# Half-tile hand-offs in attention, a re-ordered last expert quad and norm, and a ring of 19 in the second expert layer

## What is computed

```
h = concat(meta, x)                                     # 272 x 1024
layer 0: h += conv_and_gated_linear_attention(rms_norm(h))
         h += moe(rms_norm(h))
layer 1: h  = h[16:] + grouped_query_attention(rms_norm(h))   # 16 heads, 4 kv heads, 272 keys
         h += moe(rms_norm(h))
out = rms_norm(h)                                       # 256 x 1024
moe: 32 experts in 4 groups; a token takes its best group and that group's two best experts
     out += gate * (silu(x @ w_gate[e]) * (x @ w_up[e])) @ w_down[e]      # 1024 -> 256 -> 1024
```

## Time and profile before

| | us |
|---|---|
| median of 3 runs (762.96, 763.95, 767.34) | 763.95 |
| the profiled execution, its own time | 761.59 |
| its span, first to last instruction | 759.7 |
| TensorE busy | 646.2 (85%) |
| VectorE busy | 250.0 (33%) |
| ScalarE busy | 172.8 (23%) |
| moved by DMA | 233.91 MB, mean 308 GB/s |
| mean granted TensorE clock | 0.937 of full |

### The profile page before, as it was taken

One profiled execution on the slowest core, in us unless ns is written; L12 is line 12 of the kernel. 1 busy time (PEld: TensorE's weight loads), 2 busy tenths in 40 slices (PEclk: granted clock), 3 DMA queues, 4 the chain that ended last, 5 costly groups with the idle time before them and its releaser, 6 DMA issues.

```text
span 759.7 us, 10990 instructions
## 1 busy us (share of the span) xinstructions
PE 646.2 (85%) x4720; PEld 398.5 (52%) x4720; DVE 250.0 (33%) x575; ACT 172.8 (23%) x354; POOL 61.4 (8%) x43
## 2 busy tenths in 40 slices
PE   3999999988899998699589988787899787686674
PEld 3896987346566373374224345466566353244231
DVE  5255434133122332033043677713213221211204
ACT  5653350031200010010005346713111000000002
POOL 4222260000000000000003420000000000000000
PEclk9999999997999999699799999999899988888888
DMA  9760345991999999999994322069999999999991
GB/s 300 272 219 1 125 125 176 374 421 62 408 422 402 423 420 421 422 420 422 417 395 156 112 75 92 1 198 424 368 424 420 420 421 421 421 420 421 421 392 63
DMA packets 45753, 233.91 MB, mean 308 GB/s; under 512 B 4432, under 2 KB 4688, under 8 KB 23168
## 3 DMA queue, kind: packets, MB, share of 16 engines
q1 hardware_dynamic: 44864, 232.34, 76.5%
q0 software_dynamic: 832, 0.76, 0.7%
HBM read 232.02 MB, written 1.05 MB: 307 GB/s over the span
## 4 chain that ended last, share of the span: by engine, by line
PE 66%; DMA 18%; DVE 6%; SPq 4%; ACT 3%; issue 2%; DVEq 0%; ACTq 0%
PE bank L1711 11%; DMA ring<-in_moe_w_up 10%; PE bank L1775 8%; DMA tail<-in_moe_w_up 7%; PE bank L1800 7%; PE bank L1748 5%; PE bank L1408 5%; PE bank L1409 4%; PE bank L1410 4%; PE bank L1762 4%; SPq L370 4%; PE bank L1617 4%; PE bank L1863 4%; ACT scratch L832 2%; PE bank L1870 1%
## 5 line engine op out<-in xcount | busy, mean ns | idle before, releaser
L1711 PE MATMUL bank<-ring,hnT 128*32 128x256 f32 (+1 forms) x1616 | 141.5, 462 | 56.5 <-DMA ring<-in_moe_w_up 24.8
L1711 PEld LDWEIGHTS bank<-ring,hnT 128*32 128x32 f32 x1616 | 70.7, 128 | 120.8 <-issue 50.9
L1800 PE MATMUL bank<-moe_scratch 128*128 128x512 f32 (+1 forms) x160 | 78.1, 611 | 1.8 <-ACT moe_scratch L739 1.6
L1192 DVE TENSOR_TENSOR moe_scratch<-moe_scratch,bank 128x256 f32<-128x256 f32 x16 | 6.7, 421 | 182.4 <-ACT moe_scratch L733 182.4
L1172 DVE TENSOR_TENSOR h<-bank,h 128x512 f32<-128x512 f32 (+1 forms) x80 | 55.1, 689 | 23.7 <-PE bank L1800 23.7
L1775 PE MATMUL bank<-sel,hn 128*128 128x256 f32 x240 | 59.1, 406 | 0.0
L1748 PE MATMUL bank<-ring,moe_scratch 128*32 128x512 f32 x496 | 58.2, 595 | 0.3 <-ACT moe_scratch L735 0.3
L1775 PEld LDWEIGHTS bank<-sel,hn 128*128 128x128 f32 x240 | 58.0, 337 | 0.0
L1800 PEld LDWEIGHTS bank<-moe_scratch 128*128 128x128 f32 (+1 forms) x160 | 22.7, 169 | 50.3 <-issue 26.3
L1408 PE MATMUL bank<-hnT_hi,mix_hi 128*128 128x272 f32 x160 | 47.1, 294 | 1.7 <-DVE scratch L1016 1.7
L733 ACT ACTIVATE moe_scratch<-bank 128x256 f32<-128x256 f32 x16 | 6.1, 384 | 186.0 <-PE bank L1711 186.0
(11 more groups left out here) (291 smaller groups left out, 852.0 us busy)
## 6 DMA issues: line engine op xcount, KB each, us to landing
ring<-in_moe_w_down SPq DMA_DIRECT2D x62, 1024.0 KB, 25.9
ring<-in_moe_w_up SPq DMA_DIRECT2D x48, 1024.0 KB, 24.2
ring<-in_moe_w_gate SPq DMA_DIRECT2D x46, 1024.0 KB, 22.1
ring<-in_sc_w_in SPq DMA_DIRECT2D x12, 1024.0 KB, 12.5
tail<-in_moe_w_gate SPq DMA_DIRECT2D x10, 1024.0 KB, 26.2
tail<-in_moe_w_up SPq DMA_DIRECT2D x8, 1024.0 KB, 25.4
ring<-in_moe_w_gate SPq DMA_DIRECT2D x14, 512.0 KB, 9.3
ring<-in_moe_w_up SPq DMA_DIRECT2D x14, 512.0 KB, 10.1
```

Of the source, the lines that this page charges most:

```text
L1711: return mm(bank[at, :], xT[:, c, mine], right, start=(c == 0), stop=(c == KC - 1))
L1800: mm(B[[7, 4][k % 2]][0:m, :], selgT[:, TILE_AT[t]:TILE_AT[t] + m], y[:, half, :], start=True, stop=True).then_inc(sem(f"sc_ps{l}"), 1)
```

## The change

1. **Ring of layer 1.** `RING` becomes [18, 19]. The token arrays `h` and `hn` are laid side by side, with the meta tokens' tile last in `h` and first in `hn` (`ROW = [2, 1, 0]`), so that these two rows' columns form one 1 MB slot, number 18, which is unit 0 of layer 1. It is loaded once `rstd_att` is known, after which layer 1 uses meta rows no more.
2. **Last quad** (both layers). `scatter(q - 1)` and its additions come between the gate and the up products of the last quad. The last scatter goes tile by tile.
3. **Attention.** Scores, maxima, exponentials and reciprocal with scalings are handed over per query tile, in two halves; the order of the three engines' lists changes, and `att_values(p-1)` comes ahead of `turn_probs(p)`.
4. **Final norm.** In halves of 512 columns, with four output transfers of 256 KB in place of two of 512 KB; the epsilon is the root's bias.

```
-    RING, HOME = 18, 16
+    RING, HOME, SIDE = [18, 19], 16, 2
...
-                  [4, 5, 3, 8, 9, 10, 11, 12, 13, 14, 15, 6, 7, 16, 17, 0, 1, 2]]
+                  [18, 4, 5, 3, 8, 9, 10, 11, 12, 13, 14, 15, 6, 7, 16, 17, 0, 1, 2]]
...
+        with ExitStack() as both:
+            rows = both.enter_context(nc.sbuf_tensor("rows", [P, 6 * D], f32))
...
+        slots.append(rows[:, 2 * D:4 * D])
...
             def first_units1():
+                sp.wait_ge(sem("rstd_att"), 1)
+                unit(1, 0)
                 wait_mix_read(sp, 1, 2)
-                for i in range(3):
+                for i in range(1, 4):
                     unit(1, i)
                 sp.wait_ge(sem("oT_ps"), 8)
-                for i in range(3, 11):
+                for i in range(4, 12):
                     unit(1, i)
                 wait_mix_read(sp, 1, NMIX[1] - 2)
-                for i in range(11, 15):
+                for i in range(12, 16):
                     unit(1, i)
                 wait_mix_read(sp, 1, NMIX[1] - 1)
-                for i in range(15, 18):
+                for i in range(16, 19):
                     unit(1, i)
...
+                first = RING[l]
+                for i in range(first, NU):
+                    if i == first or stage_of(i - first) != stage_of(i - first - 1):
+                        sp.wait_ge(sem(f"stage_done{l}"), stage_of(i - first) + 1)
                     unit(l, i)
...
             for i in range(2):
-                sp.wait_ge(sem("hn_ready"), HN_BEFORE[4] + i + 1)
-                sp.dma_start(out[0, i * P:(i + 1) * P, :], hn[:, 1 + i, :]).then_inc(sem("out_done"), 16)
-            sp.wait_ge(sem("out_done"), 32)
+                for half in range(2):
+                    cols = slice(half * W, half * W + W)
+                    sp.wait_ge(sem("hn_ready"), HN_BEFORE[4] + 2 * i + half + 1)
+                    sp.dma_start(out[0, i * P:(i + 1) * P, cols], hn[:, 1 + i, cols]).then_inc(sem("out_done"), 16)
+            sp.wait_ge(sem("out_done"), 64)
...
+        def scattered(q, tiles):
+            if q < NQ - 1:
+                return [(half, t) for half in range(2) for t in tiles]
+            return [(half, t) for t in tiles for half in range(2)]
...
+                if n == 4:
+                    done = steps * NQ * 4 + (NQ - 1) * 4
+                    for i, t in enumerate(tiles):
+                        for half in range(2):
+                            act.wait_ge(sem("h_added1"), done + 2 * i + half + 1)
+                            cols = slice(half * W, half * W + W)
+                            nc.scalar.activation(hn[:, t, cols], h[:, ROW[t], cols], ACT.Square,
+                                                 accum_out=(stats[:, 4, 0, t:t + 1], half_ss[:, t:t + 1])[half]).then_inc(sem("norm_ss"), 1)
+                            if i == 1:
+                                act.wait_ge(sem("norm_var"), upto(4) + half + 1)
+                                of = slice(tiles[half], tiles[half] + 1)
+                                nc.scalar.activation(stats[:, 4, 2, of], stats[:, 4, 1, of], ACT.Sqrt,
+                                                     bias=eps_bias[:, 0:1], scale=1.0 / D).then_inc(sem("norm_std"), 1)
+                    return
...
-            exps(0)
+            exps(0, 0)
+            exps(0, 1)
             qT_out(1)
             for p in range(8):
-                if p < 7:
-                    exps(p + 1)
-                pT_out(p)
                 if p:
                     oT_out(p - 1)
+                if p < 7:
+                    exps(p + 1, 0)
+                pT_out(p)
+                if p < 7:
+                    exps(p + 1, 1)
...
+            def last_norm():
...
+                total(0)
+                invert_root(4, 0)
+                dve.wait_ge(sem("gain_in"), 32)
+                scaled(0, 0)
+                total(1)
+                scaled(0, 1)
+                invert_root(4, 1)
+                scaled(1, 0)
+                scaled(1, 1)
...
                     for q in range(NQ):
+                        if q == NQ - 1:
+                            add_tokens(base, q - 1)
                         dve.wait_ge(sem(f"silu{l}"), base + q + 1)
                         nc.vector.tensor_tensor(he, act_g, B[2][:, F:2 * F], ALU.mult).then_inc(sem(f"he{l}"), 1)
-                        if q:
+                        if 0 < q < NQ - 1:
                             add_tokens(base, q - 1)
...
-            invert(0)
-            qT_out(1)
             for p in range(8):
+                normalize(p, 0)
+                if p:
+                    meta_out(p - 1)
                 if p < 7:
-                    maxima(p + 1)
-                if p >= 2:
-                    oT_low(p - 2)
+                    maxima(p + 1, 0)
+                normalize(p, 1)
+                if p == 0:
+                    qT_out(1)
+                if p:
+                    oT_low(p - 1)
                 if p < 7:
-                    invert(p + 1)
-                meta_out(p)
-            oT_low(6)
+                    maxima(p + 1, 1)
+            meta_out(7)
             oT_low(7)
...
                     q = NQ - 1
-                    gate_up(r, q)
+                    gate_up(r, q, (0,))
+                    scatter(r, q - 1)
+                    gate_up(r, q, (1,))
                     he_transposes(r, q)
-                    scatter(r, q - 1)
                     transpose_weights(r, q)
                     down(r, q)
                     scatter(r, q)
...
             for p in range(8):
                 if p < 7:
-                    att_scores(p + 1)
-                turn_probs(p)
+                    att_scores(p + 1, 0)
                 if p:
                     att_values(p - 1)
+                if p < 7:
+                    att_scores(p + 1, 1)
+                turn_probs(p)
             att_values(7)
```

More of the change, by code:

```diff
@@ L83, in last_user @@
     def last_user(l, slot):
-        return max(i for i in range(NU) if RING_ORDER[l][i % RING] == slot)
+        return max(i for i in range(NU) if RING_ORDER[l][i % RING[l]] == slot)
     def landed(stage):
@@ L916, in _ @@
             link(nc.vector.memset(hn[:, 0, :], 0.0))
+            nc.vector.memset(eps_bias[:, :], EPS)
             nc.vector.memset(stats[:, :, :, :].rearrange("p a b c -> p (a b c)"), 1.0).then_inc(sem("clear"), 1)
             nc.vector.memset(z[:, :, :].rearrange("p a b -> p (a b)"), 0.0).then_inc(sem("clear"), 1)
-            norm(0)
+            first_norm()
             transposes_out(0)
@@ L1165, in add_tokens @@
                 def add_tokens(base, q):
[L1167 to L1168 removed]
+                    for k, (half, t) in enumerate(scattered(q, tiles)):
                         n = TILE_N[t]
                         dve.wait_ge(sem(f"sc_ps{l}"), (base + q) * nadd + k + 1)
[L1171 removed]
+                        hh = h[0:n, ROW[t], half * W:(half + 1) * W]
                         nc.vector.tensor_tensor(hh, B[[7, 4][k % 2]][0:n, :], hh, ALU.add).then_inc(sem(f"h_added{l}"), 1)
@@ L1368, in _ @@
                     dve.wait_ge(sem("proj_ps"), PROJ["out1"] + k + 1)
-                    hh = h[:, 1 + i, half * W:(half + 1) * W]
+                    hh = h[:, ROW[1 + i], half * W:(half + 1) * W]
                     nc.vector.tensor_tensor(hh, B[k][:, :], hh, ALU.add).then_inc(sem("h_mixed1"), 1)
             moe(1)
-            norm(4)
+            last_norm()
         @block.tensor
@@ L1653, in turn @@
                         for c in range(4):
-                            last = nc.tensor.transpose(turn_place(n, i, half)[:, c, :], h[0:m, t, 4 * half + c:D:KC], ident[0:m, 0:m])
+                            last = nc.tensor.transpose(turn_place(n, i, half)[:, c, :], h[0:m, ROW[t], 4 * half + c:D:KC], ident[0:m, 0:m])
                         last.then_inc(sem("hnT_ps"), 1)
@@ L1699, in arrived @@
                     pe.wait_ge(sem(f"weights{l}_{stage % NSEM}"), r * per + count)
-                    return [RING_ORDER[l][i % RING] for i in range(NU) if stage_of(i) == stage]
+                    return [RING_ORDER[l][i % RING[l]] for i in range(NU) if stage_of(i) == stage]
                 def wait_x(r, n):
@@ L1720, in first_gate_up, with gate_up @@
                     last.then_inc(sem(f"stage_done{l}"), 1)
-                def gate_up(r, q):
-                    for u in range(2):
+                def gate_up(r, q, parts=(0, 1)):
+                    for u in parts:
                         if q == 1 or q % 2 == 0:
@@ L1790, in scatter @@
                     pe.wait_ge(sem(f"selgT{l}"), r * NQ + q + 1)
-                    for k in range(nadd):
-                        half, t = k // NT, tiles[k % NT]
+                    for k, (half, t) in enumerate(scattered(q, tiles)):
                         m = TILE_N[t]
-                        if k == 0:
+                        if half == 0:
                             pe.wait_ge(sem(f"y_act{l}"), r * NQ + q + 1)
```

(15 more changed lines are left out.)

140 lines of the change are left out of this document (71 added, 69 removed).

## The result

| kernel | median, us | executions |
|---|---|---|
| before | 763.69 | 8, 759.52 to 767.34 |
| changed | 757.58 | 8, 754.66 to 761.90 |

The account below looks back on a forecast made before the run. Experts were taken as bound by the weight stream, attention by VectorE and ScalarE alternating, the end by norm and output transfer. Gains 3.7 + 6.1 + 2.5 + 0 + 1.3 = 13.6 us off 763.95 gave 750.3 us, range 746 to 757.

Parts of the forecast that it names:

- Layer 0's last quad: Scatter fills TensorE's wait before the up products; down products then wait for their last matrix until 387.1; gain 3.7 us.
- rival (e): Little is left: attention period near 5 us, down products at the lower clock in both layers; about 761 us; chance 0.03.
- Layer 1's last quad: Down products start at most 1.9 us earlier, but idling some 4 us lowers the clock and costs 1.9; gain 0.
- Rival (b): The clock holds in layer 1's last down product, or falls only briefly; 748.4 us; chance 0.15.
- Attention: Working in halves shortens the period and the end, less a loss at the first pair; gain 6.1 us.
- The steady period: Attention's time per pair falls from 5.02 to 4.3 us; over 7 periods this gains 5.0 us.
- the end: Attention from the start of the last turn_probs to the last values: 3.2 us instead of 5.6, gaining 2.4.
- rival (a): Attention finds a new wait: 4.7 us a pair, saving 3.3 us; kernel takes 753.1 us; chance 0.20.
- The start term: Attention's first pair gives back 1.3 us: its first turn_probs stands behind a maxima half, a second reciprocal and hops.
- The ring: Layer 1's weight stream has 77 units instead of 78 after the hole, so it ends earlier; gain 2.5 us.
- Rival (c): The 19th unit is loaded, but something else sets the end of the stream; 752.8 us; chance 0.08.
- Final norm: Tile 1's squares begin before the last addition ends, and the last output transfer is half as large; gain 1.3 us.

Follow-up runs that it names:

- after_warm: Changed kernel plus dummy products (8 in layer 0, 4 in layer 1) on TensorE ahead of the last quad's down products; 755.94 us, ratio 0.9885.
- after_qt: Changed kernel with VectorE's copy of the second half of the turned queries moved ahead of pair 1's maxima; 755.33 us, ratio 0.9876.
- only_quad: Changed kernel with the other three parts put back, keeping quad 6's scatter ahead of the last quad's up products; 762.76 us, ratio 0.9989.
- only_ring: Changed kernel with the other three parts put back to old code, keeping the ring of 19; 761.44 us, ratio 0.9971.
- both shifted kernels: Changed kernel with 32 or 64 one-column memsets ahead of VectorE's first instruction; 753.31 us (ratio 0.9855) and 751.54 us (ratio 0.9841).
- only_att: Changed kernel with the other three parts put back to old code, keeping attention's new order; 760.81 us, ratio 0.997.

## Why the prediction was wrong

The direction was right and the size was not.

- **Layer 0's last quad, forecast 3.7, measured -0.3.** The start was right: the down products wait for DMA from 383.8 on, until 388.1 (forecast 387.1). The step that failed is that I priced the lower clock for the down products of layer 1 only, 1.9 us. For layer 0 the loss was put at nothing; it stood in the bounds alone, as "lost a little to the clock", and in rival (e). The same edit makes the longer idle stretch in layer 0 (4.22 us there, 1.98 in layer 1), and there it cost 2.9 us. With the wait filled (after_warm) the down products end at 392.0, 2.4 us earlier than before. The other 1.3 us of the forecast are nearly all the start, 388.3 instead of 387.1, for the landing took over a microsecond longer than in the row.
- **Layer 1's last quad, forecast 0 (1.9 less 1.9), measured 1.7.** The down products start 0.14 us behind their landing, where it was 1.88. The wait was 1.98 us, not some 4, because the gate products took 2.8 us longer than before, with the gap of 1.46 us in them; without such a gap, in after_warm, idle time and dummies make 4.8 us. And the clock held. Rival (b) came true in this execution, by a gap that nobody had forecast, and after_warm and after_qt, with 5.34 us there, show the other case. The Trainium skill (TensorE: Matmul & The Clock Gate, "Why this matters for your kernels") has the rule that idle gaps between bursts lower the clock. I had agreed with it for layer 1; it was borne out in layer 0 (4.22 us idle, then 0.50), where I had not applied it.
- **Attention, forecast 6.1, measured 3.3.** The steady period was right (4.35 us, forecast 4.3), and so was the end (3.4, forecast 3.2); rival (a) did not come. The start term was nearly right too: the first turn_probs came 1.6 us later behind the first scores, charged were 1.3. The step that failed is that the round from the first turn_probs to the second was counted as one of seven at 4.3 us, at the full clock. It took 6.3 us at a granted clock of mostly 0.50, so it lost 1.7 us where 0.7 were to be gained: 2.4 of the missing 2.8. With the old order a stretch as long at the lower clock cost 0.3 us (48.5 in only_quad against 48.2), since TensorE has idle time in a round there; the new order leaves it none, and the forecast did not ask what the lower clock of that place would then cost. With the order of after_qt it takes 4.6 us and attention 42.4, within 0.4 of the forecast.
- **The ring, forecast 2.5.** From the end of stage 0 to the landing of the last down matrix the changed kernel took (709.02 + 27.89) - 540.12 = 196.8 us, the kernel before 741.05 - 541.96 = 199.1: 2.3 us (540.12 and 541.96 are the ends of the first stage's products on TensorE's timeline). only_ring alone gained 2.2. Rival (c) did not come. That the whole stretch gained 2.9, near the forecast of 2.5, is partly luck: the last quad added the 1.7 above, and 1.2 were lost between the output product and the end of the first stage (42.4 us against 41.3), which the prediction had put at nothing or a little. There the first stage's products ran at a granted clock of 0.50 until about 537 and took 4.4 us in place of 3.6. The other kernels with the new order need 41.2 to 42.1 us for it, so it looks like this execution's clock and not like the change.
- **Final norm, forecast 1.3, measured -1.3.** The mechanism was right, as the tail of 12.1 us in both shifted kernels shows against 13.1 before. The step that failed: nothing was put down for the time between the last addition and the norm's first operation, which was 0.52 us before and 2.81 here. Adding or taking away instructions anywhere moves the whole of VectorE's code, and the shifts show that this gap hangs on where the code lies. It cost 2.3 us.

The failed terms are 4.0 for layer 0, 2.8 for attention and 2.6 at the end, less 0.4 from the output product to the last down products. Together that is 9.0 us, the difference between 13.6 and the 4.6 between the two profiled executions. The medians are 6.1 apart; executions of one kernel spread by more than the 1.5 us between those two numbers.

## What to carry to other kernels

When an edit makes TensorE wait for a transfer instead of doing postponed work, price the burst behind the wait at the lower clock, or fill the wait with products on constants. When in-order lists are woven anew, work out the first and the last round by themselves, with the instructions that the steady ones don't need and with the clock that the trace shows there. And where an engine jumps, compare the gap behind the jump in both traces first. If it has changed, shift that engine's code by some dozens of cheap instructions and time that before judging the edit.

## What the runs showed of the hardware

- Gaps on VectorE behind a jump, with no releaser: 2.7 to 3.0 us in front of the final norm in four kernels (changed, after_warm, after_qt, only_att), 0.5 us in the two that differ from the changed one by memsets at the start alone. A shift by 32 instructions was enough. That these are loads of code is inferred from the shift; no row names it, and the packet on the instructions' queue comes without the gap too.
- 32 down products took 3.64 us in every row at full clock and 5.1 to 6.6 us after 3.6 to 4.2 us without a product. Behind 1.1 to 2.9 us without one (layer 1) it was 3.64 us in six kernels and 5.34 in two.
- A gap without a releaser lies inside TensorE's gate products of layer 1's last quad too, 0.2 us in the kernel before, up to 2.6 in the others without dummies and none in the three with them. Its cause is open.
- "issue" on the chain of waits need not be lost time: in layer 0 of the kernel before it stood at 3.02 us, of which TensorE was idle for 0.18.
